# A filter stage with its backward kernel formed in PSUM, its sine argument in turns, its basis split in place and three spectrum slots

## The reference, cut to what matters

```python
hdn = jnp.sin(sin_freq[0] * (feats @ pe_w1 + pe_b1))
hdn = jnp.sin(sin_freq[1] * (hdn @ pe_w2 + pe_b2))
k = (hdn @ pe_w3) * (jnp.exp(-t * jnp.abs(decay)) + MOD_SHIFT)
k_fwd, k_bwd = k[:, :D_MODEL], k[:, D_MODEL:]
k_circ = jnp.concatenate([k_fwd, zeros, k_bwd[:0:-1]], axis=0)
kf = jnp.fft.rfft(k_circ, axis=0)
```

## Time and profile before

| what | us |
|---|---|
| median of three runs | 3693.0 (3691.22 to 3696.77) |
| the profiled execution | 3697.59 |
| its span in the trace | 3695.8 |
| TensorE busy in the span | 3504.7 |
| first transform begins | 63.04 |
| input projection begins | 215.32 |

### The profile page before, as it was taken

The page is one execution under the profiler, slowest core; times in us unless marked ns, Lnnn a source line. Parts: engine busy times, 40 slices in busy tenths (PEclk is TensorE's granted clock), DMA queues, the critical chain, the costliest instruction groups (busy, mean ns, idle before and its releaser), DMA issues. The chain is left out here.

```text
span 3695.8 us, 47103 instructions
## 1 busy us (share of the span) xinstructions
PE 3504.7 (95%) x19104; PEld 3039.2 (82%) x19104; DVE 1540.4 (42%) x2528; ACT 1036.7 (28%) x1558; POOL 1241.4 (34%) x819
## 2 busy tenths in 40 slices
PE   7899998989999999999989998999989999999997
PEld 6888887778788888888878878888878888888886
DVE  7855544565344434444431015777340222111116
ACT  4421211233511111111342215777343111111113
POOL 5421114534422222222451304666352222222223
PEclk9899999999999999999999999999999999999998
...
GB/s 133 129 170 109 108 81 175 215 229 74 52 75 74 77 72 63 69 69 63 80 180 126 163 164 171 177 177 155 92 23 41 40 40 35 40 40 35 41 41 63
DMA packets 173814, 365.92 MB, mean 99 GB/s; under 512 B 16967, under 2 KB 98439, under 8 KB 171944
## 3 DMA queue, kind: packets, MB, share of 16 engines
...
...
## 5 line engine op out<-in xcount | busy, mean ns | idle before, releaser
L150 POOL TENSOR_TENSOR w_lo<-w_raw,w_hi 128x1024 fp32r<-128x1024 f32 x207 | 502.8, 2429 | 1451.9 <-ACT w_hi L144 1451.8
L158 PE MATMUL ps_r<-a_hi,w_hi 128*128 128x512 f32 (+1 forms) x2496 | 889.8, 356 | 18.5 <-POOL a_lo L1933 10.6
L158 PE MATMUL ps_r<-a_lo,w_hi 128*128 128x512 f32 (+1 forms) x2496 | 885.7, 355 | 0.0
L158 PE MATMUL ps_r<-a_hi,w_lo 128*128 128x512 f32 (+1 forms) x2496 | 884.3, 354 | 0.0
L158 PEld LDWEIGHTS ps_r<-a_hi,w_hi 128*128 128x128 f32 x2496 | 473.5, 190 | 95.8 <-POOL a_lo L1933 18.6
L158 PEld LDWEIGHTS ps_r<-a_lo,w_hi 128*128 128x128 f32 x2496 | 473.7, 190 | 65.4 <-issue 1.2
L158 PEld LDWEIGHTS ps_r<-a_hi,w_lo 128*128 128x128 f32 x2496 | 473.1, 190 | 66.1
L144 ACT ACTIVATE w_hi<-w_raw 128x1024 fp32r<-128x1024 f32 x207 | 217.7, 1052 | 976.7 <-PE ps_r L158 555.5
L2132 DVE TENSOR_TENSOR hid_l<-hid_l,ps_r 128x1280 f32<-128x1280 f32 x44 | 65.5, 1488 | 824.3 <-PE ps_r L158 824.3
L2152 DVE SCALAR_TENSOR_TENSOR x_t_l<-ps_r,mod,x_t_l 128x1024 f32<-128x1024 f32 (+1 forms) x288 | 241.3, 880 | 260.3 <-PE ps_r L158 260.3
L158 PE MATMUL ps_in<-x_split_f,w_hi 128*128 128x512 f32 (+1 forms) x1152 | 312.6, 359 | 4.8 <-DVE gout_f L673 4.8
...
## 6 DMA issues: line engine op xcount, KB each, us to landing
...
v_hl<-v_d SPq DMA_DIRECT2D x128, 128.0 KB, 2.9
...
```

Of the source, the lines that this page charges most:

```text
L150: pool.tensor_tensor(wl[:, s, 0:width], raw[:, s, 0:width], wh[:, s, 0:width].bitcast(F32), ALU.subtract).then_inc(w_split, 1)
L158: last = pe.matmul(out[:, c0:c1], w[:, c % 2, blk * 128:blk * 128 + 128], x[:, c0:c1], start=start and b == 0 and term == 0, stop=stop and ...
```

## The change

Within the first stage alone:

- `generate` multiplies forward taps into SBUF and backward taps in place in PSUM, 256 columns each; sum and difference then read one operand from SBUF and one from PSUM. The memset goes ahead of the product. `taps` waits for `pq_ok`, the end of `generate(g - 2)`, instead of the product's end.
- The sine argument is kept in turns: three VectorE instructions instead of six in a phase, with the factor in `ACT.Sin`'s scale.
- The basis is loaded from an array of its own into the place where its low part will stand, and split there. `raw` is free from the start, and rows run in steps 2 to 7 of the first three quarters.
- Three `gout` slots instead of two.
- `made_in` takes two tiles in step 0 and two in step 1. `w3_high` and `decay` of the quarter after the next run in step 5.
- The projection begins in `pg[1]`, and waits for the last `combine` only from its second entry on. `X_AFTER` is earlier.

```diff
-TWO_PI_HI = 6.28125
-TWO_PI_LO = 2 * math.pi - TWO_PI_HI
+TURN = 6.283185
 MAGIC = 12582912.0
...
-PQ_DVE = 40
-E_FILT, E_IN, E_FWD, E_INV, E_OUT, E_FFN, E_QKV = 10, 24, 9, 16, 8, 6 * FC, 24
+E_IN, E_FWD, E_INV, E_OUT, E_FFN, E_QKV = 24, 9, 16, 8, 6 * FC, 24
...
+            bas_raw = [place(f"basis_raw{b}", (X1, base_a + 40960)[b], [128, 5, 2, 1024]) for b in range(2)]
...
-            gout = place("gout", REST + 5120, [128, 2, 2, 256])
+            gout = [[place(f"gout{b}{side}", (REST + 5120 + 2048 * b + 1024 * side, gaps[2 + side] + 2048)[b // 2], [128, 256])
+                     for side in range(2)] for b in range(3)]
...
-            g_out = [sem(f"g_out{b}", st) for b in range(2)]
+            g_out = [sem(f"g_out{b}", st) for b in range(3)]
...
-            ROWS_AT = range(9, 9 + 2 * (16 - E_PE))
-
-            def made_pq(eng, g):
-
-                if g < PQ_DVE:
-                    eng.wait_ge(pq_v, g + 1)
-                else:
-                    eng.wait_ge(pq_p, g + 1 - PQ_DVE)
+            ROWS = {10 * q + j + 2: 6 * q + j for q in range(3) for j in range(2 * (16 - E_PE) // 3)}
+            LAST_ROW = max(ROWS)
...
-                return range(10 * q + 10 if j == 0 else 10 * q + j + 12, 10 * q + j + 13)
+                if j < 2:
+                    return range(10 * q + 10 + 2 * j, 10 * q + 12 + 2 * j)
+                return range(10 * q + j + 12, 10 * q + j + 13)
+
+            def basis_raw(j):
+                return bas_raw[j // 5][:, j % 5, 1, 0:basis_width(j)]
+
+            def pin(j):
+                return pg[(j + 1) % 2]
...
-            X_AFTER = {1: (0,), 2: (1,), 4: (2,), 5: (3,), 7: (4,), 9: (5, 6, 7)}
+            X_AFTER = {1: (0,), 2: (1,), 3: (2,), 4: (3,), 5: (4,), 6: (5,), 7: (6,), 9: (7,)}
...
+                def load_basis(j):
+                    sp.dma_start(basis_raw(j), t["filt"][j, :, 0:basis_width(j)]).then_inc(bs_in[j], 16)
+
                 sp.dma_start(cvec[:, :, :], t["cvec"]).then_inc(cv_in, 16)
                 load_early(0)
                 load_gen(0)
+                sp.dma_start(cb[:, :, :], t["crow"]).then_inc(cb_in, 16)
                 load_early(1)
-                sp.dma_start(cb[:, :, :], t["crow"]).then_inc(cb_in, 16)
                 sp.dma_start(negt[:, :], t["negt"]).then_inc(ng_in, 16)
+                load_basis(0)
                 load_early(2)
+                load_basis(1)
                 load_early(3)
-                load_entry(sp, 0, wsrc(0))
+                load_basis(2)
+                load_gen(1)
                 for m in range(4, E_PE):
                     load_early(m)
-                load_entry(sp, 1, wsrc(1))
-                load_gen(1)
+                load_basis(3)
+                load_basis(4)
+                load_row(0)
+                load_row(1)
+                for j in range(7, 10):
+                    load_basis(j)
                 for dst, src in ((par[:, :], t["par"]), (ident[:, :], t["ident"])):
                     sp.dma_start(dst, src).then_inc(c_in, 16)
-                load_entry(sp, 2, wsrc(2))
-                load_entry(sp, 3, wsrc(3))
+                sp.wait_ge(pe_c, E_PE)
+                load_basis(5)
+                load_basis(6)
...
+                basis_lo(0)
                 for g in range(10):
                     pq_low(g)
-                    if g in (1, 7):
-                        basis_lo(g // 7)
-                    if g == 4:
+                    if g in (1, 4, 7):
+                        basis_lo(g // 3 + 1)
+                    if g == 5:
                         w3_low(1)
                 for s in range(30):
-                    if s < 8:
-                        basis_lo(s + 2)
-                    if s in (8, 18):
+                    if s < 6:
+                        basis_lo(s + 4)
+                    if s in (5, 15):
...
+                decay(0)
                 sine(0, 0)
+                w3_high(0)
                 sine(0, 1)
-                w3_high(0)
-                sine(1, 0)
                 act.wait_ge(cb_in, 16)
                 act.activation(cb[:, :, :], cb[:, :, :], ACT.Silu).then_inc(cb_ok, 1)
+                sine(1, 0)
                 sine(1, 1)
+                basis_hi(0)
                 act.wait_ge(ng_in, 16)
-                decay(0)
                 for g in range(10):
                     window(g)
                     if g:
                         pq_high(g - 1)
-                    if g in (2, 8):
-                        basis_hi(g // 8)
+                    if g in (1, 4, 7):
+                        basis_hi(g // 3 + 1)
                     if g == 5:
                         w3_high(1)
+                        decay(1)
                 pq_high(9)
                 for s in range(40):
                     q, j = s // 10, s % 10
-                    if s < 8:
-                        basis_hi(s + 2)
-                    if s in (8, 18):
+                    if s < 6:
+                        basis_hi(s + 4)
+                    if s in (5, 15):
                         w3_high(q + 2)
-                    if q < 3 and j == 0:
-                        decay(q + 1)
+                        decay(q + 2)
...
+                    if s == 30:
+                        act.wait_ge(pl_ok, 40)
...
                                       fcol[0:p, layer + 2:layer + 3], ALU.add, ALU.mult).then_inc(dve_s, 1)
-                    dve.wait_ge(dve_s, 5 * n + 1)
-                    dve.tensor_scalar(c, a, 1.0 / (2 * math.pi), MAGIC, ALU.mult, ALU.add).then_inc(dve_s, 1)
-                    dve.wait_ge(dve_s, 5 * n + 2)
-                    dve.tensor_scalar(c, c, MAGIC, None, ALU.subtract).then_inc(dve_s, 1)
-                    dve.wait_ge(dve_s, 5 * n + 3)
-                    dve.scalar_tensor_tensor(a, c, -TWO_PI_HI, a, ALU.mult, ALU.add).then_inc(dve_s, 1)
-                    dve.wait_ge(dve_s, 5 * n + 4)
-                    dve.scalar_tensor_tensor(a, c, -TWO_PI_LO, a, ALU.mult, ALU.add).then_inc(dve_s, 1)
-                    dve.wait_ge(dve_s, 5 * n + 5)
-                    dve.tensor_scalar(a, a, 3.1415925, -3.1415925, ALU.min, ALU.max).then_inc(arg_ok, 1)
-
+                    dve.wait_ge(dve_s, 2 * n + 2)
+                    dve.tensor_scalar(c, a, MAGIC, None, ALU.add).then_inc(dve_s, 1)
+                    dve.wait_ge(dve_s, 2 * n + 3)
+                    dve.scalar_tensor_tensor(a, c, MAGIC, a, ALU.subtract, ALU.subtract).then_inc(arg_ok, 1)
+
+                dve.tensor_scalar(fcol[:, 2:4], fcol[:, 2:4], 1.0 / (2 * math.pi), None, ALU.mult).then_inc(dve_s, 1)
+                dve.wait_ge(dve_s, 1)
                 for layer in range(2):
                     for h in range(2):
                         phase(layer, h)
...
                     dve.wait_ge(pe_k, g + 1)
-                    ker = win[:, g % 2, :, :].rearrange("p a b -> p (a b)")
+                    fwd, bwd, tap_b = win[:, g % 2, 0, :], win[:, g % 2, 1, :], gbank(g)[:, 256:512]
                     if g % 10 in (0, 8):
-                        dve.scalar_tensor_tensor(ker, ker, 0.05, gbank(g), ALU.add, ALU.mult).then_inc(zero, 1)
+                        dve.memset(win[0:1, g % 2, 1, :], -0.05).then_inc(zero, 1)
                         dve.wait_ge(zero, g // 10 * 2 + g % 10 // 8 + 1)
-                        dve.memset(win[0:1, g % 2, 1, :], 0.0).then_inc(ker_ok, 1)
-                    else:
-                        dve.scalar_tensor_tensor(ker, ker, 0.05, gbank(g), ALU.add, ALU.mult).then_inc(ker_ok, 1)
-                    if g >= PQ_DVE:
-                        return
+                    dve.scalar_tensor_tensor(fwd, fwd, 0.05, gbank(g)[:, 0:256], ALU.add, ALU.mult)
+                    dve.scalar_tensor_tensor(tap_b, bwd, 0.05, tap_b, ALU.add, ALU.mult).then_inc(ker_ok, 1)
                     dve.wait_ge(ker_ok, g + 1)
                     if g >= 2:
                         dve.wait_ge(pl_ok, g - 1)
-                    dve.tensor_tensor(pq[:, g % 2, 0, :], win[:, g % 2, 0, :], win[:, g % 2, 1, :], ALU.add)
-                    dve.tensor_tensor(pq[:, g % 2, 1, :], win[:, g % 2, 0, :], win[:, g % 2, 1, :],
-                                      ALU.subtract).then_inc(pq_v, 1)
+                    dve.tensor_tensor(pq[:, g % 2, 0, :], fwd, tap_b, ALU.add)
+                    dve.tensor_tensor(pq[:, g % 2, 1, :], fwd, tap_b, ALU.subtract).then_inc(pq_ok, 1)
...
-                    if s >= 2:
-                        dve.wait_ge(g_out[s % 2], 32 * (s // 2))
+                    if s >= 3:
+                        dve.wait_ge(g_out[s % 3], 32 * (s // 3))
                     dve.wait_ge(odd_ok, s + 1)
                     even = bank(s)[:, 0:256]
-                    dve.tensor_tensor(gout[:, s % 2, 0, :], even, odd[s % 2], ALU.add)
+                    dve.tensor_tensor(gout[s % 3][0], even, odd[s % 2], ALU.add)
                     if j % 2 == 0:
-                        ins = dve.tensor_tensor(gout[:, s % 2, 1, :], even, odd[s % 2], ALU.subtract)
```

(13 more changed lines are left out.)

80 lines of the change are left out of this document (33 added, 47 removed).

## The result

The changed kernel takes 3657.1 us, the median of four runs (3654.5 to 3662.9), beside 3693.8 for the kernel before in runs taken with it: a ratio of 0.9903, 95% interval 0.9885 to 0.9920. The profiled execution took 3654.66 us. The forecast was 3642.6, with a range of 3636 to 3658. The kernel is faster, as said, by 36.7 us between the medians and by 42.9 between the profiled executions, where 50.4 were expected.

The account below looks back on a forecast made before the run. TensorE was busy 95% of the run, its first stage a chain with VectorE close behind. Gains of 11.8 + 8.6 + 12.4 + 7.5 + 4.5 + 5.6 = 50.4 us gave 3642.6 us beside the median 3693.0, range 3636 to 3658.

Parts of the forecast that it names:

- What bounds the stage: First stage: a chain through all engines, with VectorE next to TensorE, 29.48 of 29.90 us busy in the second quarter.
- One generation: VectorE's work on one tile in `generate`: 1.45 us instead of 1.4 not held or 2.5 held beside GpSimd.
- Opening: Before the first transform: shorter sine phases, GpSimd becomes the bound, transforms start at 51.2 instead of 63.0, -11.8 us.
- First quarter: First quarter of transforms: no basis waits, VectorE's step 3.27 against TensorE's 3.36; 29.8 us instead of 38.4, -8.6.
- Quarter boundaries: Between quarters: waits for taps' weights, tiles and rows shrink to 0.3 us; second quarter -12.4 us, third -7.5.
- Fourth quarter: Last quarter of transforms: third slot and earlier projection weights end waits; 25.5 us instead of 30.0, -4.5.
- Join: Start of projection: the 4.81 us wait for the last combine goes, 2.3 of low clock comes back; together -5.6 us.
- The reserve for late tokens: At the join, 1.5 us kept back because token blocks cost about 7.0 us a pair against 5.8 on TensorE.
- VectorE becomes the bound: Rival: VectorE held even with a PSUM operand, first-quarter step 5.5 us; 3656.9 us, chance 0.11.
- slow tail: Rival: token splits stay at 33 us, TensorE waits 3.7, fourth quarter keeps its 4.5; 3649.3 us, chance 0.13.
- The clock: Rival: TensorE stays at 1.2 GHz through the transforms, costing 88 us; 3730.6 us, chance 0.06 (0.04 slower).
- two rivals: The range's upper end, 3658, was set to reach over the tail and the VectorE case.

Follow-up runs that it names:

- u_gen: Changed kernel with the product of window and taps again one 512-column operation into SBUF, sum and difference reading two SBUF operands; 3667.5 us.
- d_row: Changed kernel with the six row products of the first quarter replaced by memsets, so three rows of the modulation are left out; 3650.5 us.
- f_tok: Changed kernel with the scaling of the odd token blocks on ScalarE instead of VectorE; 3655.3 us.
- f_x: Changed kernel with the first two token blocks requested ahead of the store of step 29, the next two ahead of that of step 30; 3656.7 us.

## Why the prediction was right, and where it was short

- **What bounds the stage**: right. The chain with VectorE next to TensorE is what the experiments move. The four parts that were undone one at a time cost 10.4, 3.0, 6.9 and 6.3 us, 26.6 of 36.7 if they add. No run undoes the basis loaded ahead, the earlier weights and rows or the tiles' order; for these the traces alone speak: ScalarE's 15.3 us of waits for basis entries and the row's 4.49 are gone.
- **One generation**: right, 1.46 against 1.45 us, never held, and in-place writing of PSUM has no surcharge (0.42). The Trainium skill's fixed longer term for a PSUM source ("VectorE: DVE Perf Modes", errata) is not seen here: 256 columns take 0.41 to 0.42 us with a PSUM source and 0.41 without, and where no semaphore stands between, the next operation starts 0.33 us behind either. Its rule that two SBUF inputs meet in contention with GpSimd ("GPSIMD Engine Reference", Key points) agrees with the sums, differences and row products above. That sentence of the Trainium skill names a second condition, which the prediction left out: VectorE in a 2-port perf mode. The tokens' scalings read one tensor from SBUF and were held as well; free, they took 1.14 us for 1280 columns, where the two-input split of as many took 1.49, so they may fall under it, but no run here shows the mode.
- **Opening**: right in size (-12.4 for -11.8), down to the first tile at 25.80 and the first transform at 50.7 (51.2 reckoned). The reason was half right: GpSimd's splits are last before transform 0, but u_gen shows VectorE as close behind them.
- **First quarter**: this is the step that failed, "1.45 + 1.15 (row product) + 0.67 (combine) = 3.27 on VectorE". I had read from the trace what is held, two operands in SBUF, and applied it to the operations that the change rewrites, not to the row product between them, whose inputs both lie in SBUF. From start to start the four held products took 8.4 us where 4 x 1.15 = 4.6 were reckoned, and GpSimd's splits stretched with them. The quarter lost 2.8 us and, by the lag, the second 2.5; d_row removes both.
- **Quarter boundaries**: the second is explained by that lag. In the third 0.82 us of a split's lag and 0.56 at the taps are left where 0.3 was reckoned. No run was made for it, but d_row bears on it: with no row product in the quarter ahead, TensorE has neither wait behind transform 10, and both (0.83, 0.57) behind transform 20. Four of the second quarter's row products took 1.32 to 1.49 us for a free 1.22.
- **Fourth quarter**: -1.3 for -4.5. I had priced a pair of token blocks (7.15 us measured, 7.0 forecast) and then not asked what the held scalings do to the combines in front of which they stand. f_tok gives back 2.1 us of this, f_x 0.5. The third slot was right and underrated: without it two quarters ahead of the fourth lose as well.
- **Join**: right. The wait and the low clock behind it are gone (1.00 in the stretch at 175.4). The reserve for late tokens was not used; another wait, 2.18 us at the first transposes behind late weights, took its place, and the prediction had not looked there.
- **Rivals**: none came as stated. "VectorE becomes the bound" gave the measured time to within 0.2 us for a wrong reason: it blamed the generations, and the rows were held. Of the slow tail the fourth quarter's part came in the main (3.2 of the 4.5 us forecast there did not come), TensorE's 3.7 us of waits for tokens did not. The clock did not turn against the change.
- **The number**: 3657.1 lies 14.5 us above the forecast and 0.9 inside the range. The upper bound was set for two rivals that did not happen as described, so that it held is in part luck; the direction and the list of parts that pay are not.
